# A two-block transformer kernel rewritten: three-product projections, splits three halves ahead, mixer work at fixed places, 2 MB expert chunks

## What is computed

```
y = sigmoid(gm) * ym + sigmoid(ga) * ya
x = rmsnorm(x + gate * (y @ w_out), final_g)
```

```
gate, idx = lax.top_k(jnp.swapaxes(aff, 1, 2), cap)      # 16 experts, cap = 32 tokens each
y = einsum(silu(xs @ w_gate) * (xs @ w_up), w_down) * gate
```

## Time and profile before

| | us |
|---|---|
| median of 3 runs (1792.33 to 1796.99) | 1793.75 |
| span of the profiled execution | 1794.1 |
| TensorE busy | 1366.5 (76%) |
| weight loads of TensorE busy | 669.3 (37%) |
| DVE busy | 496.5 (28%) |
| ACT busy | 407.6 (23%) |
| DMA | 552.69 MB, mean 308 GB/s |

### The profile page before, as it was taken

One profiled execution on the slowest core, in us unless ns is written; L12 is line 12 of the kernel. 1 busy time (PEld: TensorE's weight loads), 2 busy tenths in 40 slices (PEclk: granted clock), 3 DMA queues, 4 the chain that ended last, 5 costly groups with the idle time before them and its releaser, 6 DMA issues.

```text
span 1794.1 us, 18511 instructions
## 1 busy us (share of the span) xinstructions
PE 1366.5 (76%) x7092; PEld 669.3 (37%) x7092; DVE 496.5 (28%) x921; ACT 407.6 (23%) x619; POOL 48.5 (3%) x76
## 2 busy tenths in 40 slices
PE   4999999898999978876657666766667676767674
PEld 1877877676456457833111111111111111111110
DVE  3674345573024256541110111011101101110111
ACT  2443436663134145221101110111011101110110
POOL 1100000100010000010000000000000000000000
PEclk9999999998999988996777777777876777677767
DMA  9665567563484434365999999999999999999995
GB/s 343 192 230 186 174 214 283 208 245 117 141 300 150 140 108 161 116 246 202 418 416 416 420 419 416 416 420 418 416 416 421 418 416 417 421 417 417 417 420 209
DMA packets 142509, 552.69 MB, mean 308 GB/s; under 512 B 9288, under 2 KB 32088, under 8 KB 105472
## 3 DMA queue, kind: packets, MB, share of 16 engines
q1 hardware_dynamic: 138272, 539.00, 77.2%
q0 software_dynamic: 3632, 11.75, 1.9%
q10 hardware_dynamic: 560, 1.33, 0.2%
HBM read 550.96 MB, written 1.09 MB: 308 GB/s over the span
## 4 chain that ended last, share of the span: by engine, by line
PE 50%; DMA 21%; DVE 11%; SPq 7%; ACT 7%; issue 3%; POOL 1%; DVEq 0%; ACTq 0%; POOLq 0%
PE ps L221 31%; DMA arena<-in_w_down 18%; PE ps L1511 8%; SPq L1451 7%; PE ps L1542 5%; DVE parts L539 2%; ACT arena L250 2%; PE ps L1491 2%; DVE arena L229 2%; PE ps L1531 1%; DVE arena L237 1%; DVE arena L1607 1%; ACT parts L538 1%; DMA arena<-in_w_up 1%; ACT L1552 1%
## 5 line engine op out<-in xcount | busy, mean ns | idle before, releaser
L221 PE MATMUL ps<-parts 128*128 128x512 f32 (+2 forms) x2256 | 427.1, 350 | 26.4 <-DVE parts L539 19.7
L221 PEld LDWEIGHTS ps<-parts 128*128 128x128 f32 (+1 forms) x2256 | 359.5, 195 | 89.6 <-DVE parts L539 23.1
L1511 PE MATMUL ps<-arena 128*32 128x512 f32 x1536 | 223.8, 718 | 67.5 <-DMA arena<-in_w_up 58.7
L539 DVE TENSOR_TENSOR parts<-ring,parts 128x1024 fp32r<-128x1024 f32 x140 | 169.5, 1222 | 252.0 <-ACT parts L538 249.7
L221 PE MATMUL ps<-ring,arena 128*128 128x512 f32 (+1 forms) x480 | 192.5, 663 | 24.3 <-DMA ring<-in_w_ada 9.1
L538 ACT ACTIVATE parts<-ring 128x1024 fp32r<-128x1024 f32 x140 | 145.1, 1052 | 132.7 <-PE ps L221 117.0
L1607 DVE TENSOR_TENSOR arena<-arena,ps 128x1024 f32<-128x1024 f32 x32 | 39.1, 1221 | 410.4 <-PE ps L1542 410.4
L1531 PE MATMUL ps<-arena 128*32 128x512 f32 x512 | 110.5, 953 | 53.8 <-DMA arena<-in_w_down 42.8
L1511 PEld LDWEIGHTS ps<-arena 128*32 128x32 f32 x1536 | 48.1, 126 | 224.1 <-DMA arena<-in_w_up 112.7
L1531 PE MATMUL ps<-ring,arena 128*32 128x512 f32 x512 | 92.7, 824 | 45.0 <-DMA ring<-in_w_down 45.0
L221 PEld LDWEIGHTS ps<-ring,arena 128*128 128x128 f32 (+1 forms) x480 | 76.9, 181 | 131.0 <-issue 92.8
(11 more groups left out here) (115 smaller groups left out, 776.0 us busy)
## 6 DMA issues: line engine op xcount, KB each, us to landing
arena<-in_w_up SPq DMA_DIRECT2D x112, 1024.0 KB, 13.8
arena<-in_w_gate SPq DMA_DIRECT2D x80, 1024.0 KB, 19.1
ring<-in_w_in SPq DMA_DIRECT2D x74, 1024.0 KB, 5.4
arena<-in_w_down SPq DMA_DIRECT2D x64, 1024.0 KB, 18.8
ring<-in_w_down SPq DMA_DIRECT2D x64, 1024.0 KB, 19.2
ring<-in_w_gate SPq DMA_DIRECT2D x48, 1024.0 KB, 24.3
ring<-in_w_ada SPq DMA_DIRECT2D x36, 1024.0 KB, 5.7
ring<-in_w_up SPq DMA_DIRECT2D x16, 1024.0 KB, 25.7
```

Of the source, the lines that this page charges most:

```text
L221: return PE.do(lambda e: e.matmul(out_, lhsT, rhs, start=start, stop=stop, skip_group_check=True), after, signal)
L539: m = V.fill(place_v, lambda e: e.tensor_tensor(lo, v, hi.bitcast(F32), ALU.subtract), (h,))
L1511: ins = e.matmul(ps[32 * n:32 * n + 32, 2 + c // KD, :], XT[:, k % 2, 32 * (k // 2):32 * (k // 2) + 32], slot[:, n * W:(n + 1) * W], start ...
```

## The change

The kernel is written anew around explicit tables; every engine's program is a plain Python loop with no queue object.

- `SLOTS` lists 45 slots of 512 columns in order, with kind T (transposed) or N (natural), and `HALVES` their 188 halves of 256 rows. All projections now use the three fp32r products. The order of slots changes: q, k and v of the mLSTM alternate, the mixing gates (GM, GA) come before o and z, and the last w_out and w_out_2 halves are interleaved by column slot. The last four halves run tile by tile.
- Weight splits use four buffers; ACT and DVE split half g + 3 while TensorE is at half g. The operands of the six projections that were fp32 are split too.
- Every piece of mixer work has a place (slot, half) behind which each engine does its part. One modulation chunk follows half 3 of slots 1 to 28.
- Block 1's shift and scale: x is first on SP's queue, the eight chunks go to their own buffers, and 128 matmuls with a 128x128 piece of w_ada stationary and one moving column make the columns directly.
- Experts: 12 chunks of 2 MB, 128 rows of 16 KB, through nine slots. SP loads the first at fixed events. The expert loops are unrolled. Expert 0 is copied, not added, to the accumulator.
- Bias and gain rows of the modulation are prepared on the host in layout only and applied in place.

```diff
-SLOT = 2048
-RING = 4
-HALF = SLOT // 2
-NHALF = 3
+SLOTS = (
+    ("Q0", "T", "w_in", QM, "H"), ("V0", "N", "w_in", VM, "H"), ("K0", "T", "w_in", KM, "H"), ("V1", "N", "w_in", VM + W, "H"),
...
+NWS = 4
+AHEAD = 3
...
+NCH = 12
+E_SLOTS = 9
...
-        def plain_natural(lhs, ktiles, w, c0, ready, evac):
...
-                    for kk in range(4):
-                        m = mm(ps[:, pair[t], :], lhs(4 * q + kk, t), slot[:, kk, :], at_ == 0 and kk == 0,
...
+                if kind == "N":
+                    for t in ts:
+                        bank, tok = pair_of(s)[t], slice(t * P, (t + 1) * P)
+                        for kk in range(2):
+                            k = 2 * kp + kk
+                            mm(ps[:, bank, :], lh[:, k, tok], hi[:, kk, :], first and kk == 0, False)
+                            mm(ps[:, bank, :], lh[:, k, tok], lo[:, kk, :], False, False)
+                            ins = mm(ps[:, bank, :], ll[:, k, tok], hi[:, kk, :], False, last and kk == 1)
...
+            for k in range(KD):
+                e.wait_ge(S(f"ada0_{k}"), 16)
+                for i in range(16):
+                    ins = mm(ps[:, 7, i:i + 1], ADA0[k][:, i * P:(i + 1) * P], cst[:, k:k + 1], k == 0 and i == 0, k == KD - 1)
...
+            for g, ts in UNITS:
+                half(g, ts)
+                s, c = HALVES[g][4]
...
+                if 13 <= s < 21 and c == 0:
+                    attn_flips(s - 13)
+                if 14 <= s < 22 and c == 0:
+                    attn_values(s - 14)
+                if 12 <= s < 20 and c == 1:
+                    attn_scores(s - 12)
...
+            def hi(g):
+                if g >= NHALF:
+                    return
+                e.wait_ge(*landed(("w", g // 2)))
+                if g >= NWS:
+                    e.wait_ge(*half_done(g - NWS))
+                slot = ring[LOAD_AT["w", g // 2] % RING]
+                copy(WHI[g % NWS], slot[:, 2 * (g % 2):2 * (g % 2) + 2, :], to=S("a_hi"))
...
+            for g in range(NHALF):
+                s, c = HALVES[g][4]
+                hi(g + AHEAD)
...
+                if 12 <= s < 20 and c == 2:
+                    attn_logits(s - 12)
+                if 12 <= s < 20 and c == 3:
+                    attn_maps(s - 12)
...
-            return w_[e_, (c % KD) * P:(c % KD + 1) * P, :]
-            return wd[e_, (c - 2 * KD) * 2 * P:(c - 2 * KD + 1) * 2 * P, :].rearrange("(k p) n -> p k n", p=P)
+                return w_[e_, 256 * (c % 4):256 * (c % 4) + 256, :].rearrange("(p b) n -> p (b n)", b=2)
+            return dram["w_down"][e_, 512 * (c - 8):512 * (c - 8) + 512, :].rearrange("(p b) n -> p (b n)", b=4)
...
+            e.wait_ge(*full("RV1"))
+            e.wait_ge(*free("QF1"))
+            expert_load(0)
+            e.wait_ge(*full("CBb"))
+            expert_load(1)
...
+            e.wait_ge(*full("WP1b"))
+            expert_load(5)
+            expert_load(6)
+            expert_load(7)
+            e.wait_ge(S("v_h2"), NT)
+            expert_load(8)
+            for c in range(E_SLOTS, NE * NCH):
+                e.wait_ge(S("p_use"), c - E_SLOTS + 1)
+                expert_load(c)
```

More of the change, by code:

```diff
@@ L115, in constants @@
     return {"const": one, "early": early, "late": late}
[L118 to L164, removed]
@@ new lines, with _loads @@
+_halves()
+NHALF = len(HALVES)
+NWS = 4
+AHEAD = 3
+HALF_COUNT = [sum(1 for h in HALVES[:g + 1] if not h[3]) for g in range(NHALF)]
+UNITS = [(g, (0, 1)) for g in range(NHALF - 4)] + [(g, (t,)) for t in range(NT) for g in range(NHALF - 4, NHALF)]
+NADA = 28
+ADA_LAST = {7: "R1", 11: "R2", 19: "R3", 27: "R4"}
+ADA_STEP = {(a + 1, 3): a for a in range(NADA)}
+RING = 4
+LOADS = []
+def _loads():
+    place = {}
+    for g in range(0, NHALF, 2):
+        for gg in (g, g + 1):
+            place[HALVES[gg][4]] = g // 2
+    after = {}
+    for step, a in ADA_STEP.items():
+        after.setdefault(place[step], []).append(a)
+    for c in range(NHALF // 2):
+        LOADS.append(("w", c))
+        for a in after.get(c, ()):
+            LOADS.append(("ada", a))
@@ L168, in build @@
+def build(nc, dram, out):
     ctx = ExitStack()
     with ctx:
[L170 to L178, removed]
@@ L253, in acopy @@
-        def acopy(o, a, after=()):
-            return act(o, a, ACT.Copy, after=after)
-        def now(q):
-            return (q.sem, q.count)
-        loads = [0]
-        def load(dst, src, after=(), queue=None):
-            s = sem(f"load{loads[0]}")
-            loads[0] += 1
-            q = queue or G
-            q.wait(*after)
-            q.items.append(lambda e: e.dma_start(dst, src).then_inc(s, 16))
-            return (s, 16)
-        landed = [sem(f"landed{i}") for i in range(RING)]
@@ new lines, in build, with part, row @@
+        WIF = [small(KD, 2 * MH, dtype=F32R) for _ in range(2)]
+        def part(v, table_, name, rows=P):
+            s, n = table_[name]
+            return v[0:rows, s:s + n]
+        def row(name):
+            a, m = ROWS[name]
+            return dram["rows"][a:a + m]
+        ident, iota, causal = (part(const, CONST, n) for n in ("ident", "iota", "causal"))
+        cw = part(cols, COLS, "conv_w").rearrange("p (j c) -> p j c", j=4)
+        cb, mg = part(cols, COLS, "conv_b"), part(cols, COLS, "mnorm_g")
@@ new lines, in half_done, with ring_free, landed @@
+        def half_done(g):
+            s, kp, first, last, step = HALVES[g]
+            return full(SLOTS[s][0] + "b") if last else (S("p_half"), HALF_COUNT[g])
+        def ring_free(i):
+            what, n = LOADS[i]
+            if what == "w":
+                return S("v_lo"), 2 * n + 2
+            if n in ADA_LAST:
+                return full(ADA_LAST[n])
+            return S("p_ada"), n + 1 - sum(1 for a in ADA_LAST if a < n)
+        def landed(what):
+            i = LOAD_AT[what]
+            return S(f"ring{i % RING}"), 16 * (i // RING + 1)
```

2686 lines of the change are left out of this document (1522 added, 1164 removed).

## The result

The changed kernel takes 1775.13 us (median of four executions, 1771.46 to 1777.07) beside 1793.04 for the kernel before: ratio 0.990, 95% interval 0.988 to 0.992. Forecast was 1739, range 1702 to 1773. So the direction was right and the gain a third of the forecast one, 18 us for 54.

The account below looks back on a forecast made before the run. Bounds: TensorE before the experts, the weight stream in them. Start +32.7, products -35.2, clock -7, idle -18.7, routing +3.2, starting -1, deeper buffer -15.1, row length -13.5, tail -0.3: -54.9, to 1739 us; range 1702 to 1773.

Parts of the forecast that it names:

- Seven more for everything else: Projections and mixers: 7 us of TensorE idle outside attention, block 2's flips and the group norm; idle 35 in all.
- the rival that ends slower: Split pipeline starves TensorE: each of 43 slots loses 3.02 us, idle 130, total time 1834 us; chance 0.05.
- The seven terms of the path: Attention, from scores to transposes: splits, DVE, ACT and map times, about 11.4 us against TensorE's 9.4, 2.3 waiting per head.
- The clock term: Projections and mixers: less idle means fewer half-clock stretches; a quarter of at most 28 us, so 7 us saved.
- products: Six full-fp32 projections as three fp32r products: 0.699 us for 0.882 over 192 products, 35.2 us off the path.
- Start: Block 1's shift and scale by one-column products at low clock, 0.223 us a record: first projection at 76.5, 32.7 later.
- the first rival: Full clock at the start: one-column products take 0.12 us, 26 us less, 1713 us; chance 0.22.
- Routing: Between projections and experts: tile 1's norm ends 12.8 us after the last product, not 9.7; 32.8 becomes 36.
- my step by 4 KB: Expert weight stream: 152.2 ns more per added 4 KB of row gives 615.7 for 16 KB, 426 GB/s, 901 us.
- The second: Fixed places cost what they save: idle 54 to 75 us, mostly attention and retention, 1758 to 1779 us; chance 0.15.
- The fourth: Expert weight stream: 16 KB rows bring nothing, mean stays 417.4 GB/s, total time 1753 us; chance 0.13.
- the third: Split pipeline starves TensorE: 3.02 us lost in each of 43 slots, idle 130, total time 1834 us; chance 0.05.

Follow-up runs that it names:

- two ahead: Weight splits made two halves ahead in place of three, against the changed kernel: 1727.0 us, 0.964 of the kernel before.
- last kernel: Changed kernel with splits two halves ahead, old start, attention values in bank 4, bias row's evacuation early, decay tables one step earlier: 1672.0 us, 0.933.
- one ahead: Changed kernel with splits one half ahead in place of three, and the first scale and shift made as in the kernel before: 1709.7 us, 0.954.

## Why the prediction was wrong, step by step

**Where it failed: the depth taken for cover.** The step reads "TensorE has three halves and an ada chunk, 9.4. So 2.3 us wait in each of 8 heads, 18 us. The splits themselves stay in time" and then "Seven more for everything else: idle 35". I counted the three halves only as lead. The step does say that "ACT's split of half g+3 waits for TensorE to finish half g-1", and then gives this wait no time in the sum. With four buffers a split three ahead can't start before half g-1 is done, so it stands in ScalarE's queue, and VectorE's behind it, until TensorE has got that far, and every copy or map placed behind it is late by the split's own time. The wait comes back only as a reason for the rival that ends slower, priced at the longest old stall in each slot. The runs price it: 48 us for the depth, 32 for the wait on half g-1 alone, 16 for what is left, the place in the queue. (The seven terms of the path add up to 11.24 us, not to 11.4, so the step's own wait was 2.1 a head; it changes little.)

Idle time of TensorE in the stretch, from the order of time, in us:

| where | forecast | changed kernel | two ahead | last kernel |
|---|---|---|---|---|
| attention | 18 | 25.0 | 9.0 | 3.2 |
| block 2's flips | 5 | 7.0 | 4.3 | 4.3 |
| group norm and its splits | 5 | 3.7 | 3.5 | 3.4 |
| everything else | 7 | 30.6 | 18.4 | 8.5 |
| of it the gates' product | | 6.9 | 4.9 | 0 |
| of it retention (slots from 679 to 717) | | 12.0 | 7.3 | 2.7 |
| sum | 35 | 66.3 | 35.3 | 19.4 |

So the second step that failed is "Seven more for everything else": 24 of the 31 us too few are there. The depth explains part of it (30.6 falls to 18.4 with two ahead); the gates and the decay tables in retention stood behind other work of VectorE at either depth, and moving them is what took these away. Attention has 3.35 us a head (1.55 and 1.8) in place of 2.3. That two ahead meets my 35 is a coincidence: half my wait in attention, and more than twice my seven elsewhere.

**The clock term had the wrong sign.** I gave "a quarter, 7" back to the clock for less idle. Idle rose and the clock fell to 0.94, from 0.96 before. Busy time came out 11.3 us above the forecast: the 7 did not come, and 4.3 more went. It is dearest in attention: behind the pair of waits at 307.46 and 309.81 TensorE ran 8 us at 0.63. Over the same 3530 records, busy time is 669.8 with 66.3 idle in the changed kernel, 655.2 with 35.3 two ahead, 645.5 with 19.4 in the last kernel: a microsecond of idle went with about half another. A line through all eleven kernels whose stretch I read has the same slope, 0.49 (an estimate), ten of them within 4 us of it; one ahead lies 7 below, 650.4 busy with 47.3 idle. So where the waits fall counts too, and the half is a mean and no rule.

**Right: products.** I had 0.699 us for three fp32r products in place of 0.882 for two fp32 records. The changed kernel's records of w_out and the context projections, at full clock:

```profile
616.86 30.19 PE L519 MATMUL ps<-b,b 128*128 128x512 f32 x132
```

That is 0.686 a product; over 192 products 38 us, for my 35.

**Start: the choice right, the price a little high.** I took 0.223 us a record because the clock would be low. It was: the trace has it full from 15.6 to 19.0 us and then at half until 73.6, with TensorE busy without a pause up to 67.1. The pace followed it. From one record's start to the next it is 0.112 us while the clock is full and 0.213 from 22 to 66 us; all 256 took 51.5. So 6 us of the forecast were a price of 0.223 for 0.213, and some thirty records that ran at the full clock.

In five of the eight profiles with this start the stretch from 30 to 50 us shows 1.00, and the records took longer, 54.6 us. Two ahead is one of them:

```profile
15.96 54.61 PE L519 MATMUL ps<-b,b 128*128 128x1 f32 x256
```

From 16 to 30 us, the changed kernel and then two ahead:

```profile
16.00:30.00 14.00, 14.00 (x80) 14.00 (x80) 0.75 (x5) 0.00 (x0) 0.00 (x0) 0.61 1.01 394
16.00:30.00 14.00, 14.00 (x68) 14.00 (x67) 1.04 (x7) 0.00 (x0) 0.00 (x0) 1.00 1.01 396
```

This 1.00 can't be read as a full clock. The five traces have no clock record before 78 to 80 us, and their pace from 16 us on is 0.213, that of the half clock in the changed kernel. Their first projection starts like the changed kernel's at 0.50: 4, 7 and 7 records touch its first three microseconds in both, and 10 or 11 each microsecond once the clock is full. So I take it that the clock was at half there too; it is inferred from the pace, not recorded.

So the first rival, full clock and 26 us less, was right in its price (0.12 for 0.112) and failed in its condition: the clock didn't stay up. The Trainium skill's advice to keep TensorE busy (TensorE: Matmul & The Clock Gate, Why this matters for your kernels) is not borne out for this stream: in the changed kernel the clock fell while TensorE was 100% busy and stayed at 0.50.

**Routing: 32.2 for 36.** The 3 us that I added for the later tile don't show; why stays open. Experts: within 4 us, by two errors that cancel, the stream 9 us faster and its start 6 slower. The rate was 428 where my step by 4 KB gave 426 and I took 424; rows of 16 KB are worth 23 us (I had 13.5), nine slots in place of six 13.5 (I had 15.1). Starting took 10.8 for 5: from 832 to 843 the DMA engines moved 1 GB/s, all slots being full.

**Rivals.** The second, "fixed places cost what they save", with 54 to 75 us of idle in attention and retention and 1758 to 1779, is what happened: 66.3 us of idle, 37 of them in attention and retention. I gave it 0.15, and against it stood "three halves of lead", the very depth that caused the greater part. The fourth (16 KB rows bring nothing) and the third (130 us of idle, slower) are out. The range ended at 55 of idle although this rival reached to 75.

**Not settled.** Why the clock fell, or by the pace never rose, under a stream of one-column products without a pause; and how the 16 us of the split's place divide between late weights and the order itself: no run has three ahead with a fifth buffer.

## What to carry to other kernels

A prefetch distance equal to the ring minus one makes the producer wait for the consumer's last step, and everything queued behind the producer waits with it; leave one buffer of slack (distance 2 of 4 was the best of 1, 2 and 3 here), or count that wait for each item behind it. Where a queue mixes work ahead of time with evacuations, ask for each evacuation what stands directly before it and what that waits for. Price short waits of TensorE with the clock that goes after them, in the mean half as much again here. And list the waits of a rewritten order place by place: a lump for "everything else" was the worst term of this sum.

## What the runs showed of the hardware

Products with a 128x128 fp32 stationary operand and one moving column take 0.112 us a record at the full granted clock and 0.213 at half, in a stream of 256. The clock fell to half at 19.0 us with TensorE busy without a pause, and stayed there to the stream's end at 67.1. The Trainium skill (TensorE: Matmul & The Clock Gate, LDWEIGHTS (loading the stationary operand)) has a formula for the weight load that gives an estimate of 128/1.2, 107 ns, for 128 columns; the records at the full clock are near it, those at half take twice that.

A granted clock of 1.00 in a view can mean that the trace has no clock record there. The pace of like instructions tells: 68 records in 14 us at a shown 1.00, 80 at 0.61.

The weight stream of the experts moved 412 GB/s with rows of 4 KB, 421 with 8 and 428 with 16; with the size of the transfer doubled and the rows as before it stayed at 417.
